# One wait for the four tensors of a turn, one for each half of attention's transposes, in TensorE's queue

## The chip, the cores and the metric

The program runs on one core of a Trainium2 chip (trn2). The metric is device time in microseconds (us) of one execution, shown as the median of a few. The core has five engines with a queue of instructions each: TensorE (PE; its weight loads are shown as PEld), VectorE (DVE), ScalarE (ACT), GpSimd (POOL) and SyncE (SP), which only issues transfers. They meet through semaphores: an instruction that is done adds one to a counter, and a queue that waits for a value stands still until the counter has it, with all that is behind it.

## What is computed

The reference runs two transformer blocks over one sequence of 1024 tokens with 1024 features, all in float32. What matters here is the first block's mixer, which has two branches from the same input:

```python
def one_block(args):                       # latent attention, 8 heads, 96 features per head
    s = (jnp.einsum('bqhd,bkhd->bhqk', qn_b, k_nope)
         + jnp.einsum('bqhd,bkd->bhqk', qr_b, k_rope))
    p = jax.nn.softmax(s.astype(jnp.float32) * scale, axis=-1)
    return jnp.einsum('bhqk,bkhd->bqhd', p.astype(v.dtype), v)
...
def step(state, inp):                      # wkv7 recurrence, 8 heads of 64, run forward and backward
    sa = jnp.einsum('bhvk,bhk->bhv', state, a_t)
    state = (state * w_t[:, :, None, :] + sa[..., None] * b_t[:, :, None, :]
             + v_t[..., None] * k_t[:, :, None, :])
    return state, jnp.einsum('bhvk,bhk->bhv', state, r_t)
```

The rest (input projections, output projections, gated feed-forward, a second block with a 31-tap convolution and a squared-relu MLP) is dense matrix work that the change does not touch.

## The kernel before

The kernel is one program, written engine by engine: every function ends in the engine that it writes for (`_pe`, `_dve`, `_act`, `_pool`, `_sp`), and each engine's queue is filled in the order of the calls. Nothing is reordered by a tool. `X.up(...)` names the increment that an instruction makes when done, and `e.wait_ge(*X.by(...))` waits for it. There is one counter for each engine and part (`v` is VectorE's and `a` ScalarE's of one direction of the recurrence, `t_at`, `v_at`, `a_at` are attention's), so waiting for a later increment of an engine covers all its earlier ones.

The stage in question, `scan_pe` and its fellows, runs from about 525 to 1195 us. It interleaves three programs by a fixed table of slots (`slots`, with the orders written out in `STEADY`, `HEAD`, `ENDING`):

- direction 0 and direction 1 of the recurrence (`w_pe`, `w_dve`, ...), each in 8 steps of 128 tokens, so 16 half steps. A half step is a chain of calls: `split`, `cum`, `mul`, `turn`, `scores`, `PV`, `Nc`, the `row`s, `spread`, `X`, `Y3` to `X5`, `WU`, `RG`, `OH`, `S0`, `S1`, `post1` to `post3`. Direction 1 is 13 slots behind direction 0.
- attention (`att_pe`, ...), 64 units of one head and 128 queries: `S` (scores, line 1784), `M` and `R` on VectorE (maximum, reciprocal), `E` and `P` on ScalarE (exponential, scaling, into `Pb`), `T0` and `T1` on TensorE (four transposes of `Pb` each, line 1807, into `bank[6]`), `C0` and `C1` on ScalarE (copies into `PT`, lines 1824 and 1839), `V` (line 1795).

In `cum`, TensorE makes the running sums of the decays (lines 1367 to 1370) and ScalarE their exponentials (lines 1518 to 1527). In `mul`, VectorE makes four 128x512 tensors one after the other: At (line 1589), Rt (1594), Bt (1596) and Kt (1597). In `turn`, TensorE transposes each by four 128x128 transposes (line 1379), 16 in all, and in ScalarE's `turn` the results are copied to SBUF (lines 1536 and 1541). `scores` (line 1392) needs those copies.

The recurrence's results go through `wring`, a ring of four PSUM banks that both directions share. `wtake` takes the next bank, and waits until whoever read that bank's last content is done (line 1342). A turn takes all four banks. For direction 1 those four are left by `OH` and `cum` of its own step; for direction 0 they are left by its `cum` (three) and by direction 1's `X`, whose four copies ScalarE makes (line 1352), and that one is the bank of Kt. In direction 1's first step the fourth bank is left by direction 0's matmuls of line 1433, which VectorE adds up (line 1654).

In front of a matmul one wait can sit on the weight load itself; every further one becomes an instruction of its own in TensorE's queue, EVENT_SEMAPHORE, which holds up to two waits. By the profile's operands the wait written first is the one on the weight load, and the later ones become EVENT_SEMAPHOREs in front of it.

Of the kernel before, what the change touches and what calls it, by code (L numbers as in the profile page):

```python
# [213 lines left out]
def build(nc, A, out):  # L214
# [3 lines left out]
    def sb(name, kb, shape, dt=F32):  # L218
        return nc.alloc_sbuf_tensor_at(name, shape, dt, offset=base + int(kb * 1024))
# [6 lines left out]
    def signals(name):  # L226
        everything.append(Signals(nc, name))
        return everything[-1]
# [9 lines left out]
    def hs(h):  # L238
        return slice(512 * h, 512 * (h + 1))
# [1099 lines left out]
    def wtake(e, d, s, name, *empties):  # L1339
        ap, waits = wring.take((d, s, name), *empties)  # L1340
        for w in waits:
            e.wait_ge(*w)
        return ap
# [11 lines left out]
    def w_pe(e, d, s, c):  # L1355
        x, t, v, a, g = D[d], t_w[d], v_w[d], a_w[d], g_w[d]
# [13 lines left out]
                m = e.matmul(b2[:, 2 * p:2 * p + 2], sg[:, 128 * p:128 * (p + 1)], K("ones2", 2), start=True, stop=True)  # L1370
            m.then_inc(*t.up(s, "D"))
        if c == "turn":
            for name, sig, empty in (("At", v, a), ("Rt", v, a), ("Bt", v, a), ("Kt", v, a)):
                ap = wtake(e, d, s, name, (empty, s, name + "T"))
                e.wait_ge(*sig.by(s, name))
                for p in range(4):
                    src = {"At": x.AP[:, p, 0, :], "Bt": x.SC[:, p, 4, :, :].rearrange("t h c -> t (h c)"), "Rt": x.Rt[:, 128 * p:128 * (p + 1)],
                           "Kt": x.Kt[:, 128 * p:128 * (p + 1)]}[name]
                    m = e.transpose(ap[:, 128 * p:128 * (p + 1)], src, ident)  # L1379
                m.then_inc(*t.up(s, name))  # L1380
# [14 lines left out]
        if c == "PV":  # L1395
            e.wait_ge(*v.by(s, "SC", 1, 1))
            ap = wtake(e, d, s, "PV", (a, s, "PV"))
# [6 lines left out]
        if c == "X":  # L1404
            ap = wtake(e, d, s, "X", (a, s, "X", 3))
            e.wait_ge(*v.by(s, "XT0"))
            across_pe(e, ap, x.XT).then_inc(*t.up(s, "X"))
        if c in ("Y3", "Y4", "Y5"):
# [5 lines left out]
            ap = wtake(e, d, s, ("Y", lev), (v, s, "Y", lev))  # L1414
# [5 lines left out]
            if lev > 3:  # L1420
                ap = wtake(e, d, s, ("XT", lev - 1), (a, s, "XT", lev - 1, 3))
                across_pe(e, ap, x.X).then_inc(*t.up(s, "XT", lev - 1))
        if c in ("X3", "X4", "X5"):
# [5 lines left out]
            if lev < 5:  # L1429
                ap = wtake(e, d, s, ("X", lev), (v, s, "X", lev))  # L1430
# [5 lines left out]
            else:  # L1436
                ap = wtake(e, d, s, ("XT", lev), (v, s, "XT", lev))
# [47 lines left out]
        if c in ("S0", "S1"):  # L1485
# [8 lines left out]
            ap = wtake(e, d, s, ("S", n), (v, s, "S+", n))  # L1494
# [255 lines left out]
    PT = sb("PT", 24, [128, 8, 2, 128])  # L1750
# [7 lines left out]
    t_at, v_at, a_at = signals("t_at"), signals("v_at"), signals("a_at")  # L1758
# [15 lines left out]
    def att_pe(e, u, c):  # L1774
        g, k, j, h = u // 2, u // 16, (u // 2) % 8, u % 2
        if c == "S":
            if u % 16 == 0:
                e.wait_ge(*d_kp.by(k))
            if h == 0:
                e.wait_ge(*d_qb.by(g))  # L1780
            if u:
                e.wait_ge(*a_at.by("E", u - 1))
            for half in range(2):
                m = e.matmul(bank[4 + half], Qb[g % 3][:, h, :], Kp[k % 2][:, h, hs(half)], start=True, stop=True)  # L1784
            m.then_inc(*t_at.up("S", u))
        if c == "V":
            w = g - 1
            e.wait_ge(*a_at.by("PT", 2 * w + 1))
            if w % 8 == 0:
                e.wait_ge(*d_vp.by(w // 8))  # L1790
            if w % 4 == 0 and w:
                e.wait_ge(*a_at.by("O", w - 1))
            for i in range(8):
                for n in range(2):
                    m = e.matmul(bank[7][64 * n:64 * n + 64, 128 * (w % 4):128 * (w % 4) + 128],  # L1795
                                 Vp[(w // 8) % 2][:, i, 64 * n:64 * n + 64], PT[:, i, n, :], start=i == 0, stop=i == 7)
            m.then_inc(*t_at.up("O", w))
        if c in ("T0", "T1"):
            w, n = u - 1, int(c[1])
            e.wait_ge(*a_at.by("P", w))  # L1800
            if n:
                e.wait_ge(*a_at.by("PT0", w))
            elif w:
                e.wait_ge(*a_at.by("PT", w - 1))
            for q in range(4):
                i = 4 * n + q
                m = e.transpose(bank[6][:, 128 * q:128 * (q + 1)], Pb[w % 2][:, 128 * i:128 * (i + 1)], ident)
            m.then_inc(*t_at.up("PT", w, n))
# [166 lines left out]
    def scan_pe(e):  # L1975
        e.wait_ge(*v_pre.all())
        e.wait_ge(*a_pre.all())
        e.wait_ge(*v_gt.all())
        scan(e, "pe", w_pe, att_pe, tail_pe)
# [1500 lines left out]
```

## Time and profile before

| | us |
|---|---|
| median of the runs shown (3155.31 to 3159.33) | 3156.21 |
| the profiled execution | 3153.93 |
| its span, first to last instruction | 3152.1 |
| TensorE busy | 3069.7 (97%) |
| VectorE busy | 2026.5 (64%) |
| ScalarE busy | 1136.5 (36%) |
| mean granted TensorE clock | 0.992 of full |

Times in the rows are in us from the span's start unless marked ns. A busy TensorE is not one at its peak: matmuls overlap, so a row's length is longer than its share of the queue. What a group costs is the distance from its start to the next group's start.

### The profile page before, as it was taken

How to read it: one execution, taken by the hardware profiler on the slowest of the kernel's cores; microseconds unless marked ns; L12 is line 12 of the kernel's file. 1: busy time of each engine (PE TensorE's matmuls, PEld its weight loads, DVE VectorE, ACT ScalarE, POOL GpSimd, SP SyncE). 2: the span in 40 equal slices, each digit the busy share in tenths (PEclk: the TensorE clock that was granted, in tenths of full speed). 3: DMA queues.
4: the chain of work that ended last, by engine and by line, in shares of the span. 5: the costliest groups of instructions: out<-in, count | busy, mean ns of one | idle time of the engine just before them, and what ended most of it. 6: DMA issues, size and time to landing. Idle time of an engine off the chain costs nothing.

```text
span 3152.1 us, 52318 instructions
## 1 busy us (share of the span) xinstructions
PE 3069.7 (97%) x22008; PEld 2495.9 (79%) x22008; DVE 2026.5 (64%) x3073; ACT 1136.5 (36%) x1691; POOL 448.5 (14%) x488
## 2 busy tenths in 40 slices
PE   8999999899999999999999999999999999999999
PEld 7887887677777777888888888888766887788887
DVE  6665554477777765546555565788887888664454
ACT  5222334566666653223222222201154233433232
POOL 0232442011111100402222212101000000200000
PEclk9999999999999999999999999999999999999999
DMA  4332766223232222425455553666411222223322
GB/s 151 127 133 84 229 224 205 67 78 95 78 93 73 81 99 92 154 86 220 175 197 196 195 200 134 253 240 264 176 67 54 94 97 90 94 94 121 107 94 80
DMA packets 121754, 424.98 MB, mean 135 GB/s; under 512 B 15536, under 2 KB 41776, under 8 KB 94128
## 3 DMA queue, kind: packets, MB, share of 16 engines
q1 hardware_dynamic: 86880, 295.26, 26.6%
q0 software_dynamic: 34640, 126.37, 10.9%
q8 instruction: 175, 2.87, 0.4%
q14 instruction: 59, 0.48, 0.0%
HBM read 311.48 MB, written 110.10 MB: 134 GB/s over the span
## 4 chain that ended last, share of the span: by engine, by line
PE 81%; DVE 11%; issue 2%; ACT 2%; POOL 2%; DMA 1%; SPq 0%; DVEq 0%; ACTq 0%; POOLq 0%
PE ps L2634 30%; PE ps L321 14%; PE ps L505 7%; PE ps L2442 4%; PE ps L1784 3%; PE ps L2344 3%; PE ps L1417 2%; PE ps L2158 2%; PE ps L1379 1%; DVE st_m L1813 1%; PE ps L1433 1%; PE ps L1795 1%; PE ps L2801 1%; PE ps L1026 1%; DVE Yh L2823 1%
## 5 line engine op out<-in xcount | busy, mean ns | idle before, releaser
L293 ACT ACTIVATE whi<-raw 128x2048 fp32r<-128x2048 f32 x131 | 250.5, 1912 | 389.0 <-PE ps L2634 195.3
L297 DVE TENSOR_TENSOR wlo<-raw,whi 128x2048 fp32r<-128x2048 f32 x131 | 301.7, 2303 | 86.0 <-ACT whi L293 85.7
L2823 DVE SCALAR_TENSOR_TENSOR Yh<-uT,vc,Yh 128x512 f32<-128x512 f32 x448 | 326.2, 765 | 3.2
L2634 PE MATMUL ps<-Hh,whi 128*128 128x512 f32 x1024 | 316.9, 391 | 0.6 <-DVE wlo L297 0.6
L2634 PEld LDWEIGHTS ps<-Hh,whi 128*128 128x128 f32 x1024 | 192.2, 188 | 42.5 <-issue 1.9
L321 PE MATMUL ps<-Hlo,whi 128*128 128x512 f32 x672 | 206.9, 389 | 0.0
L321 PE MATMUL ps<-Hhi,wlo 128*128 128x512 f32 x672 | 206.9, 389 | 0.0
L321 PE MATMUL ps<-Hhi,whi 128*128 128x512 f32 x672 | 206.8, 389 | 0.0
L2634 PE MATMUL ps<-aHh,whi 128*128 128x512 f32 x512 | 199.5, 390 | 2.3 <-DVE wlo L297 2.2
L2634 PE MATMUL ps<-Hh,wlo 128*128 128x512 f32 x512 | 199.2, 389 | 0.0
L2634 PE MATMUL ps<-aHh,wlo 128*128 128x512 f32 x512 | 199.2, 389 | 0.0
L2634 PE MATMUL ps<-aLh,whi 128*128 128x512 f32 x512 | 199.2, 389 | 0.0
L3001 DVE TENSOR_TENSOR xT<-ps,xT 128x512 f32<-128x512 f32 x256 | 168.8, 682 | 20.4 <-PE ps L2634 20.4
L2634 PE MATMUL ps<-Gh,whi 128*128 128x512 f32 x576 | 180.8, 395 | 0.0
L505 PE MATMUL ps<-Hhi,whi 128*128 128x512 f32 (+1 forms) x512 | 163.5, 401 | 0.0
L505 PE MATMUL ps<-Hlo,whi 128*128 128x512 f32 (+1 forms) x512 | 158.7, 391 | 0.0
L505 PE MATMUL ps<-Hhi,wlo 128*128 128x512 f32 (+1 forms) x512 | 158.3, 390 | 0.0
L2987 DVE TENSOR_TENSOR aLh<-rth,aHh 128x512 fp32r<-128x512 f32 x64 | 43.0, 713 | 164.1 <-ACT aHh L2981 164.1
L321 PEld LDWEIGHTS ps<-Hhi,wlo 128*128 128x128 f32 x672 | 126.2, 188 | 26.2
L321 PEld LDWEIGHTS ps<-Hlo,whi 128*128 128x128 f32 x672 | 126.2, 188 | 26.1
L321 PEld LDWEIGHTS ps<-Hhi,whi 128*128 128x128 f32 x672 | 126.2, 188 | 26.1
L1784 PE MATMUL ps<-Kp,Qb 96*128 96x512 f32 x256 | 125.9, 614 | 5.9 <-ACT Pb L1829 4.5
(415 smaller groups left out, 6470.0 us busy)
## 6 DMA issues: line engine op xcount, KB each, us to landing
raw<-in_panels SPq DMA_DIRECT2D x131, 1024.0 KB, 4.8
whi<-sph SPq DMA_DIRECT2D x28, 1024.0 KB, 4.8
wlo<-spl SPq DMA_DIRECT2D x28, 1024.0 KB, 6.9
rwf<-F POOLq DMA_DIRECT2D x16, 1280.0 KB, 6.7
sraw<-in_panels POOLq DMA_DIRECT2D x40, 512.0 KB, 4.5
sph<-shi POOLq DMA_DIRECT2D x40, 512.0 KB, 4.5
spl<-slo POOLq DMA_DIRECT2D x40, 512.0 KB, 5.2
L<-rwf SPq DMA_DIRECT2D x16, 1024.0 KB, 5.0
```

What stands on the lines that cost most here:

```text
L293: e.activation(whi[i % 2][:, :], raw_of(i)[:, :], AF.Copy).then_inc(*a_hi.up(i))
L297: e.tensor_tensor(wlo[i % 2][:, :], raw_of(i)[:, :], whi[i % 2][:, :].bitcast(F32), OP.subtract).then_inc(*v_lo.up(i))
L321: m = e.matmul(aps[h][0:n1 - n0, :], w[wi][:, kc, n0:n1], mov[mi][:, kc, hs(h)], start=x == 0 and q == 0, stop=x == len(kcs) - 1 and q == 2)
L505: m = e.matmul(aps[h][0:n1 - n0, :], W[wi][:, kc, n0:n1], H2[mi][:, kc, hs(h)], start=kc == 0 and q == 0, stop=kc == 7 and q == 2)
L1417: m = e.matmul(ap[cols(cc_), 32 * i:32 * (i + 1)], x.SC[cols(cc_), p, BA, h, :], part(x.X[cols(cc_), i, :], lev, d), start=True, stop=True)
L1784: m = e.matmul(bank[4 + half], Qb[g % 3][:, h, :], Kp[k % 2][:, h, hs(half)], start=True, stop=True)
L2158: m = e.matmul(aring.bank("ya", n, h), W[wi][:, k, n0:n0 + 128], (oahi, oalo)[mi][:, k, hs(h)], start=k == 0 and q == 0, stop=k == 3 and q ...
L2344: m = e.matmul(aps[h], W[wi][:, kc, n0:n0 + 128], H2[mi][:, kc, hs(h)], start=kc == 0 and q == 0, stop=kc == 7 and q == 2)
L2442: m = e.matmul(ap, W[wi][:, kc, 128 * n:128 * n + 128], (aH, aL)[mi][b % 2][:, kc, :], start=kc == 0 and q == 0, stop=kc == 1 and q == 2)
L2634: m = e.matmul(ap, W[wi][:, kc, n0:n0 + 128], mov[mi][:, kc, :], start=x == 0 and q == 0, stop=x == len(kcs) - 1 and q == 2)
L2823: e.scalar_tensor_tensor(out=to, in0=x, scalar=w, in1=to, op0=OP.mult, op1=OP.add).then_inc(*v_e.up(*key))
L3001: e.tensor_tensor(xT[:, n, hs(h)], ring.bank("x", h, b, n), xT[:, n, hs(h)], OP.add).then_inc(*v_e.up("x", h, b, n))
```

## The change

Two places in TensorE's queue. In `turn`, the four waits for At, Rt, Bt and Kt, one in front of each tensor's transposes, become one wait for Kt, the last that VectorE makes, in front of all; and all four banks are taken ahead of the first transpose instead of one by one. In `T0` and `T1`, the wait for `P` goes where a later increment of the same counter is waited for anyway. The instructions that compute, their order and the data are the same.

```diff
         if c == "turn":
-            for name, sig, empty in (("At", v, a), ("Rt", v, a), ("Bt", v, a), ("Kt", v, a)):
-                ap = wtake(e, d, s, name, (empty, s, name + "T"))
-                e.wait_ge(*sig.by(s, name))
+            e.wait_ge(*v.by(s, "Kt"))
+            aps = {name: wtake(e, d, s, name, (a, s, name + "T")) for name in ("At", "Rt", "Bt", "Kt")}
+            for name, ap in aps.items():
                 for p in range(4):
...
         if c in ("T0", "T1"):
             w, n = u - 1, int(c[1])
-            e.wait_ge(*a_at.by("P", w))
             if n:
                 e.wait_ge(*a_at.by("PT0", w))
-            elif w:
-                e.wait_ge(*a_at.by("PT", w - 1))
+            else:
+                e.wait_ge(*(a_at.by("PT", w - 1) if w else a_at.by("P", w)))
```

## Rows read from the trace of the kernel before

**Rows 1.** The page, part 1: busy time of each engine.

```profile
PE 3069.7 (97%) x22008; PEld 2495.9 (79%) x22008; DVE 2026.5 (64%) x3073; ACT 1136.5 (36%) x1691; POOL 448.5 (14%) x488
```

**Rows 2.** Busy time by stretch: length, each engine busy (instructions), granted clock, DMA share, GB/s.

```profile
591.00:1158.00 567.00, 545.98 (x9840) 434.20 (x9839) 395.52 (x866) 348.12 (x663) 53.42 (x75) 1.00 0.26 78
```

**Rows 3.** Waits of TensorE, 525 to 1155 us: in total, times, longest.

```profile
PE ps L1807 <- ACT PT L1839: 4.0, 8, 0.5
PE ps L1807 <- ACT PT L1824: 3.9, 5, 0.8
PE ps L1379 <- DVE AP L1589: 3.9, 7, 1.0
```

**Rows 4.** Timeline of a turn of direction 1: start, length, instructions.

```profile
737.67 0.68 DVE L1589 SCALAR_TENSOR_TENSOR AP<-L,E 128x512 f32<-128x512 f32 x1
738.50 0.63 PE L1379 MATMUL ps<-cc,AP 128*128 128x128 f32 x4 [0.22 <-DVE AP L1589]
739.47 0.68 DVE L1597 TENSOR_TENSOR Kt<-L,E 128x512 f32<-128x512 f32 x1
740.30 0.63 PE L1379 MATMUL ps<-cc,Kt 128*128 128x128 f32 x4
740.76 0.60 PE L1807 MATMUL ps<-cc,Pb 128*128 128x128 f32 x4
741.20 1.02 PE L1784 MATMUL ps<-Kp,Qb 96*128 96x512 f32 x2
```

**Rows 5.** Timeline of the stage's first turn, direction 0.

```profile
534.95 0.60 PE L1379 MATMUL ps<-cc,AP 128*128 128x128 f32 x4
...
536.70 0.60 PE L1807 MATMUL ps<-cc,Pb 128*128 128x128 f32 x4
```

**Rows 6.** Timeline of a later turn of direction 0.

```profile
699.36 1.59 ACT L1352 ACTIVATE X<-ps 64x256 f32<-64x256 f32 x4
699.48 0.66 PE L1379 MATMUL ps<-cc,AP 128*128 128x128 f32 x4 [0.22 <-ACT E L1523]
...
700.30 0.68 DVE L1597 TENSOR_TENSOR Kt<-L,E 128x512 f32<-128x512 f32 x1
701.13 0.63 PE L1379 MATMUL ps<-cc,Kt 128*128 128x128 f32 x4
...
701.72 0.48 PE L1417 MATMUL ps<-X,SC 64*64 64x32 f32 x10
```

**Rows 7.** The stage's second turn, direction 1, in the timeline.

```profile
588.86 1.11 PE L1379 MATMUL ps<-cc,AP 128*128 128x128 f32 x4
```

**Rows 8.** Wait instructions of lines 1375 and 1802: ns min/median/max, first and last.

```profile
L1375 PEldq EVENT_SEMAPHORE  x63: 51/51/51, 534.5 to 1143.5; - x63
L1802 PEldq EVENT_SEMAPHORE  x64: 51/51/51, 530.8 to 1149.6; - x64
```

**Rows 9.** Timeline: VectorE and TensorE waiting for each other, and a starved group of transposes.

```profile
744.18 2.48 DVE L1602 TENSOR_TENSOR SC<-ps,cc 128x512 f32<-128x512 f32 x4 [2.19 <-PE ps L1392]
...
746.72 1.15 PE L1401 MATMUL ps<-L,SC 64*64 64x64 f32 x32 [0.70 <-DVE SC L1602]
...
725.70 0.69 DVE L1662 COPY WU<-ps 128x512 f32<-128x512 f32 x1 [1.80 <-PE ps L1450]
...
726.16 0.63 PE L1807 MATMUL ps<-cc,Pb 128*128 128x128 f32 x4 [0.51 <-ACT PT L1839]
```

**Rows 10.** The chain that ended last, in order of time: start, length, what.

```profile
738.50 2.43 PE ps L1379 x16
```

**Rows 11.** Two long gaps of TensorE, in the timeline.

```profile
562.52 2.29 PE L1784 MATMUL ps<-Kp,Qb 96*128 96x512 f32 x4 [2.49 <-ACT Pb L1829]
...
2685.61 0.50 PE L2634 MATMUL ps<-aHh,whi 128*128 128x512 f32 x1 [1.84 <-DVE wlo L297]
```

**Rows 12.** Busy time by stretch behind those gaps; the clock is the third number from the end.

```profile
564.00:567.40 3.40, 3.40 (x28) 2.66 (x28) 2.04 (x3) 0.40 (x1) 1.46 (x3) 0.51 0.10 29
2685.50:2689.00 3.50, 3.39 (x15) 2.81 (x16) 3.06 (x4) 2.79 (x3) 2.84 (x2) 1.00 0.71 225
```

## The prediction

> **What bounds the kernel now.** I read the page's busy times first. TensorE is busy 97% of the span [rows 1], so whatever keeps its queue standing is paid in full unless a later wait shrinks by as much. Then the stretches: in the 567 us from 591 to 1158 us, where 14 of the 16 turns and nearly all of attention lie, TensorE is busy 546 us at full granted clock, VectorE 396 and ScalarE 348 [rows 2]. Only 21 us are idle there, and the list of waits names a few places; two of them are the places of this change: the transposes of At wait for VectorE's first multiplication, and attention's transposes wait for ScalarE's copies [rows 3].
>
> Then the timeline around a turn. The reader is to compare the times at which VectorE's multiplications start with the times at which TensorE's groups of four transposes start. In a turn of direction 1, At's multiplication starts at 737.67 and ends at 738.35, and the transposes start at 738.50; Kt's starts at 739.47 and ends at 740.15, and its transposes start at 740.30 [rows 4]. TensorE follows VectorE 0.15 us behind, tensor by tensor: three groups from 738.50 to 740.30 are 0.60 us apart, VectorE's pace. The first turn shows TensorE's own pace, since the multiplications were long done: four groups take 536.70 - 534.95 = 1.75 us, 0.44 each [rows 5]. Seven turns look like rows 4, seven like those of direction 0 [rows 6], and two, the first of each direction, find all four tensors ready [rows 5, 7].
>
> Last, the chain that ended last. It runs through the turn, 16 transposes in a row [rows 10], with VectorE's multiplication of At ahead of it and attention's and the scores' matmuls behind it.
>
> **The change part by part: the turn.** The new wait sits in front of At and ends when Kt is ready. So the 12 transposes of At, Rt and Bt, which TensorE now makes while VectorE works on the next tensor, all come behind Kt's multiplication.
>
> Direction 1: Kt is ready at 740.15 [rows 4]. How soon the first transpose follows: 0.15 us where the wait is an instruction of its own, as now; 0.06 where a single wait sits on the weight load (VectorE's fourth result ends at 744.18 + 2.48 = 746.66, the matmul starts at 746.72 [rows 9]). By the rule of the program's operands the wait for Kt, written first, now sits on the load, so I take 0.09, and 0.06 to 0.15 as bounds. First transpose at 740.24, 1.75 us for 16, next group at 741.99. Before, it started at 740.76. The loss is 1.23 us (1.20 to 1.29).
>
> Direction 0: Kt is ready at 700.98 [rows 6]. The bank for Kt is held by direction 1's X, whose copies end at 699.36 + 1.59 = 700.95, which before held back only Kt's group and now holds back all; it ends just before Kt does, so it adds nothing here, but the two are in a dead heat. Start 0.12 us behind, 701.10, then 1.75 us, and 0.09 for the change of shape in front of the 64x64 group (701.72 - 701.13 = 0.59 against 0.44 plus waiting): 702.94 against 701.72. The loss is 1.22.
>
> Fourteen turns at 1.23 us are 17.2 us. The stage's first turn loses nothing. In the second, the bank that Kt takes is left by matmuls right in front of it, so the transposes, which started at 588.86 [rows 7], now wait for a VectorE addition: 0.4 to 0.8 us, I take 0.6.
>
> What hides it: nothing that I can find. Behind the turn stand attention's T1 and S, then the scores, and those are followed by a VectorE wait of 2.19 us and by TensorE's next wait of 0.70 us for VectorE's products [rows 9]. Both hang on TensorE's own scores and move with them. ScalarE's copies of a turn now start about 1 us later, still in front of the scores that read them, because the four 512-column matmuls of S stand between [rows 4], or the small matmuls of line 1417 in direction 0 [rows 6]. VectorE's next multiplications are no fixed point either: 12 us ahead of them, at 725.70, VectorE stood 1.80 us waiting for TensorE's matmuls of line 1450 [rows 9] and worked on from there almost without a gap, so it moves with TensorE and at the next turn the same wait is met again. The transfer that reloads the inputs waits for Bt and Kt, which don't move. The bounds are full price, and half of it if some later wait gives way.
>
> **The waits themselves.** Dropped from the turn: three waits on VectorE. Four banks are waited for by two instructions ahead. That is 63 instructions less and about 32 more. Dropped in attention: 64 + 63 = 127. Each instruction lasts 51 ns [rows 8]. Are they paid? In rows 4 the group at 740.76 has two waits in front, and it starts 0.46 us behind the last; a group with nothing late takes 0.44 [rows 5]. TensorE's queue reads the waits while earlier matmuls still run, so a wait that is over costs 0 to 0.02 us: I take nothing. Where the wait is late, it stands in the way: removal moves the release from a separate instruction onto the load, 0.05 us (one instruction) to 0.09 us (0.15 less 0.06). That applies to the starved groups, 8 + 5 in the list of waits [rows 3] (one of them is the group at 726.16 [rows 9]) and, as an estimate, one more that waits for P. 14 x 0.07 = 1.0 us gained. Upper bound of this part: all of 158 - 32 less at 51 ns, taken under the last rival.
>
> Beside this, the Trainium skill ("Advanced Engine Details and Errata", Network/Comms) gives 50 to 100 ns for a sequencer to read a semaphore. By it, if nothing overlapped, 127 reads would be an estimated 6 to 13 us; the 0.46 against 0.44 us above speaks against that here.
>
> **TensorE's clock.** A turn's gap grows: in direction 1 from 0.22 or 0.96 to some 2.0 or 2.7 us, in direction 0 to 1.8 us behind one group of four transposes. Gaps of that size are on either side of trouble: behind the one of 2.49 us that ended at 562.52 the granted clock was half (1.2 instead of 2.4 GHz) for some 3.4 us, behind the one of 1.84 us that ended at 2685.61 it stayed full [rows 11, 12]. Between the two lie all of the new gaps, with thin work around those of direction 0. A stretch of 3.4 us at half clock costs at most 1.7 us; the row of four transposes at 588.86, in another such stretch, is 1.11 us long against 0.60 at full clock [rows 5, 7]; not all of 3.4 us is such work, so I take 1.5 us. I expect 5 of the 14 turns to be hit: 7.5 us; bounds 0 and 14 x 1.7 = 24 us.
>
> The Trainium skill ("Perfetto Trace Analysis", Matmul Optimizations) says that the engine "dynamically scales power based on utilization", so that matmuls should run back to back in batches. A batch of 16 in place of four of four looks like that advice, but the gap in front is longer than all it closes; the rows above carry the price.
>
> **Sum.** 17.2 + 0.6 - 1.0 + 7.5 = 24.3 us. On the profiled execution's own 3153.93 that is 3178.2. The median of the runs is 2.28 us above it, so 3180.5.
>
> **Rivals.**
> - *The delay alone.* The new gaps leave the clock at full: 3156.2 + 16.8 = 3173.0. For it: the clock is 1.00 over 567 us although gaps up to 1.0 us are in it. Against: the row of 2.49 us.
> - *Nearly every turn loses the clock.* 16.8 + 22 = 3195.
> - *The delay is absorbed.* Later waits of TensorE give way by half: 3156 + 8 = 3164, fully: 3156. For it: 0.70 and 0.51 us waits exist. Against: they hang on TensorE's own work, and the chain goes through the turn.
> - *Other side: the waits cost their 51 ns, and turns lose nothing.* Then 127 + 31 = 158 instructions at 0.051 us are 8.1 us, 3148. It decides only if VectorE had Kt ready when TensorE comes to the turn, as in rows 5; in 14 turns of 16 Kt is 1.6 us or more late. A mechanism that is there only in the two first turns.
>
> **How the numbers follow.** Delay with some clock loss 55%, delay alone 25%, nearly every turn at half clock 7%, absorbed 8%, waits dear and turns free 5%. The range leaves out the last and the deep end of absorption: 3168 (delay alone with a quarter absorbed) to 3196. Slower by over 0.2% is all but the last two, and a part of absorption: 92%; within 0.2% (6.3 us, about what a measurement can tell from no change) 4%; faster 4%.
>
> **What would show it.** In every turn of rows 4 and 6 the first transpose starts just behind the end of Kt's multiplication and the 16 run 0.44 us a group; the wait of TensorE at line 1379 grows from about 5 us in total to 25 to 30, by VectorE's Kt (line 1597). The next groups are 1.2 us later against VectorE's At than before. Starved groups of line 1807 start 0.05 to 0.09 us sooner after ScalarE. The page's clock line and the stretch from 591 to 1158 us show the half clock as a mean below 1.00: five stretches are 0.985. The rest of the program, from 1196 us on, takes as long as before. I am wrong if the stage does not lengthen (some wait gives way that I took to hang on TensorE), if the transposes start before Kt is ready, or if X's copies in direction 0 end later than Kt and hold all 16 back still more.

## The result and the profile after

The changed kernel is slower: 3176.10 us, median of 4 runs (3170.79 to 3184.63), against 3155.76 for the kernel before (4 runs, 3150.22 to 3159.33). The ratio is 1.0062, 95% interval 1.0044 to 1.0081. Five more runs later, beside the last experiment, gave 3174.83 against 3153.92, ratio 1.0068 [1.005, 1.0085]. The forecast was 3180.5, range 3168 to 3196. The profiled execution took 3170.79, its span is 3169.0.

The page, part 1, of the kernel after. TensorE is busy 3.5 us less than in [rows 1], in a span 16.9 us longer, so it stands idle 20.4 us more:

```profile
PE 3066.2 (97%) x22008; PEld 2498.1 (79%) x22008; DVE 2026.0 (64%) x3073; ACT 1137.1 (36%) x1691; POOL 447.9 (14%) x488
```

Waits of TensorE in the kernel after, 525 to 1175 us (total, times, longest). The diff makes all later lines of TensorE one smaller, so line 1806 is line 1807 of before, and so on:

```profile
PE ps L1379 <- DVE Kt L1597: 29.0, 14, 2.7
...
PE ps L1806 <- ACT PT L1823: 3.4, 5, 0.7
PE ps L1806 <- ACT PT L1838: 2.9, 7, 0.4
...
PE ps L1379 <- DVE X L1654: 0.6, 1, 0.6
```

Where [rows 3] had 3.9 us for At in 7 turns, there are now 29.0 us for Kt in 14. The two waits for ScalarE's copies went down from 4.0 and 3.9 us to 2.9 and 3.4. The second turn waits 0.6 us for an addition of VectorE.

A turn of direction 1 in the kernel after, timeline, to be laid beside [rows 4]:

```profile
829.54 0.68 DVE L1597 TENSOR_TENSOR Kt<-L,E 128x512 f32<-128x512 f32 x1
...
830.28 0.66 PE L1379 MATMUL ps<-cc,AP 128*128 128x128 f32 x4 [2.02 <-DVE Kt L1597]
...
830.77 0.60 PE L1379 MATMUL ps<-cc,Rt 128*128 128x128 f32 x4
...
831.21 0.60 PE L1379 MATMUL ps<-cc,SC 128*128 128x128 f32 x4
...
831.64 0.60 PE L1379 MATMUL ps<-cc,Kt 128*128 128x128 f32 x4
...
832.08 0.60 PE L1806 MATMUL ps<-cc,Pb 128*128 128x128 f32 x4
```

Kt's multiplication ends at 830.22. The first transpose starts 0.06 us behind it, the next group 1.86 us behind it. In [rows 4] that group started 0.61 us behind Kt's end (740.76 - 740.15), so the turn loses 1.25 us. A turn of direction 0, as the chain of the work that ended last passes through it (start, length, what):

```profile
786.58 0.51 DVE AP L1589
...
787.18 0.40 DVE Rt L1594
...
787.78 0.69 DVE SC L1596
788.47 0.61 DVE Kt L1597
789.08 0.08 issue
789.16 1.94 PE ps L1379 x16
791.10 0.99 PE ps L1417 x30
```

In [rows 10] VectorE's part of the chain ended with At; now it runs through all four multiplications and only then come the sixteen transposes. TensorE and VectorE, which worked side by side, work one behind the other.

The same instruction of VectorE can be found in both traces by its number in the queue. The distance between the two, from one instruction to the next, shows where time is lost. Worked out from the two traces, 620 to 1150 us of before:

```
start before  start after  step us  turn of direction
   622.86        624.27     +2.90     0   (and +1.51 more up to 627)
   664.25        668.43     +1.25     1
   702.88        709.90     +2.84     0
   744.18        752.40     +1.25     1
   782.74        792.20     +1.25     0
   824.07        835.50     +1.26     1
   862.62        876.89     +2.83     0
   903.94        920.99     +2.85     1
   942.49        962.38     +2.84     0
   984.53       1005.62     +1.25     1
  1023.81       1047.73     +2.84     0
  1066.07       1090.97     +1.24     1
  1105.43       1133.09     +2.83     0
  1145.76       1174.64     +1.29     1
```

Fourteen steps, each at a turn. Seven are the delay alone, 1.25 us. In the other seven half clock stands behind it and costs some 1.6 us more (2.84 - 1.25), at the first of them 3.2. Apart from one of 0.75 us (a gap of TensorE at 797.20 for which the trace names no wait) nothing else in this stretch stays that is larger than about 0.3 us. The sum is 14 x 1.25 = 17.5 for the delay, 6 x 1.59 + 3.2 = 12.7 for the clock, and 0.75: 31 us (the distance itself goes from -1.5 at 620 us to +28.9, so small steps give back 0.6). Of the 28.9, 16.9 are left at the end. By TensorE's own instructions the distance falls to 19.4 at 1196 us: the kernel before had its own stretches of half clock from 1158 us on, 27 us long in all, the kernel after only 6.8 there, and 20.5 us less of half clock can be worth up to 10.2. The other 2.5 go at about 1313 us, where TensorE stands 2.2 us waiting for VectorE (line 2344) in the kernel before and not at all in this execution. The second trace of the changed kernel has a wait of 2.3 us there again, so the change doesn't bring that gain.

Timeline of one of the seven turns with half clock, and busy time by stretch of two of them and of the turn shown above (length, each engine busy, granted clock third from the end):

```profile
914.17 1.12 PE L1379 MATMUL ps<-cc,AP 128*128 128x128 f32 x4 [2.02 <-DVE Kt L1597]
...
915.07 1.06 PE L1379 MATMUL ps<-cc,Rt 128*128 128x128 f32 x4
```

```profile
914.00:917.40 3.40, 3.23 (x15) 3.24 (x16) 1.75 (x7) 1.57 (x3) 1.45 (x3) 0.51 0.71 216
1043.80:1047.20 3.40, 3.40 (x34) 3.07 (x32) 0.00 (x0) 2.78 (x5) 0.00 (x0) 0.50 0.91 296
830.00:833.40 3.40, 3.12 (x23) 2.64 (x24) 1.87 (x7) 2.43 (x5) 1.45 (x3) 1.00 0.73 243
```

The two turns at 914 and at 830 have the same gap of 2.02 us in front. The reader is to see that one of them is followed by half clock (0.51 of full, 1.2 GHz) and the other by full clock: the length of the gap alone does not decide it. At half clock the groups of a turn stand 0.85 to 0.90 us apart instead of 0.44.

### The profile page after: what moved, and what is told of

Same layout as the page of the kernel before. It is cut to its first block, busy times and chain, and to the rows that moved or that the text cites. A ratio compares the mean times of both kernels' runs of the same rounds, so it can differ in the third digit from the quotient of the medians.

```text
span 3169.0 us, 52160 instructions
## 1 busy us (share of the span) xinstructions
PE 3066.2 (97%) x22008; PEld 2498.1 (79%) x22008; DVE 2026.0 (64%) x3073; ACT 1137.1 (36%) x1691; POOL 447.9 (14%) x488
## 4 chain that ended last, share of the span: by engine, by line
PE 81%; DVE 12%; issue 2%; ACT 2%; POOL 1%; DMA 1%; SPq 0%; DVEq 0%; ACTq 0%; POOLq 0%
PE ps L2633 30%; PE ps L321 14%; PE ps L505 7%; PE ps L2441 4%; PE ps L2343 3%; PE ps L1784 3%; PE ps L1417 2%; PE ps L2157 1%; PE ps L2280 1%; PE ps L1379 1%; DVE st_m L1812 1%; PE ps L2800 1%; PE ps L1026 1%; DVE Yh L2822 1%; PE ps L1795 1%
```

## The experiments

Each kernel was timed in turns with the kernel before on the same chip; the medians of the latter stand beside each.

**Attention's waits alone.** The turn is as before; only the edit in `T0` and `T1` is made.

```diff
-            e.wait_ge(*a_at.by("P", w))
             if n:
                 e.wait_ge(*a_at.by("PT0", w))
-            elif w:
-                e.wait_ge(*a_at.by("PT", w - 1))
+            else:
+                e.wait_ge(*(a_at.by("PT", w - 1) if w else a_at.by("P", w)))
```

> Only the waits of T0 and T1 are changed; the turn is that of the kernel before. Late-Kt theory (the turn's twelve transposes behind Kt cost the time): this part is worth 0.05 to 0.09 us for each of some 14 starved groups, so 1 us less than before, within what can be told from no change; the 943 ns gaps of attention's second group in the first steps shrink by 0.09 us. Rival (each wait instruction costs its 51 ns): 127 instructions, 6.5 us faster. Rival (something in attention's waits made the changed kernel slow): 10 us or more slower.

3155.18 us (12 runs, 3144.73 to 3159.89) against 3158.16; ratio 0.9995 [0.9977, 1.0012]. Its waits, 525 to 1175 us:

```profile
PE ps L1379 <- DVE AP L1589: 4.3, 7, 1.0
...
PE ps L1806 <- ACT PT L1823: 3.4, 5, 0.7
PE ps L1806 <- ACT PT L1838: 2.9, 7, 0.4
```

127 wait instructions of 51 ns [rows 8] are gone, 6.5 us if they were paid one by one, and by the ratio the time went down by 1.6 us (0.05%), inside an interval that reaches to 7.3 us gained; the fit below narrows it to 0.8 +- 1.5. What is gained is seen at the starved groups: those that wait for the second copy stood 4.0 us in 8 places [rows 3], now 2.9 in 7; one by one, seven of them wait 0.42 instead of 0.51 us and five of those for the first copy 0.69 instead of 0.78, in sum 12 x 0.09 = 1.1 us. The turn waits for At as before. This half of the change is free of harm and nearly of use.

**The turn alone.** Attention's waits are as before, the turn as after.

> Only the turn is changed; attention's waits are those of before. Late-Kt theory: as the changed kernel plus 1 us, so some 20 us slower than before, 1.25 us at each of 14 turns and the rest from stretches at half clock. Rival (attention's waits made the difference): within 6 us of before.

3185.60 us (6 runs, 3169.55 to 3187.72) against 3158.16; ratio 1.0091 [1.0059, 1.0123]. The turn alone has the whole loss. That it comes out 9 us above the whole change goes with the mean granted clock of its runs, 0.9877 against 0.9898; at equal clock the two are 16.2 +- 2.2 and 14.9 +- 1.8 us above the kernel before (table below).

**All four banks first, each tensor with its own wait.**

```diff
-            for name, sig, empty in (("At", v, a), ("Rt", v, a), ("Bt", v, a), ("Kt", v, a)):
-                ap = wtake(e, d, s, name, (empty, s, name + "T"))
-                e.wait_ge(*sig.by(s, name))
+            aps = {name: wtake(e, d, s, name, (a, s, name + "T")) for name in ("At", "Rt", "Bt", "Kt")}
+            for name, ap in aps.items():
+                e.wait_ge(*v.by(s, name))
```

> All four banks are taken ahead of the first transpose, but each tensor keeps its own wait on VectorE. Late-Kt theory: nothing lost in direction 1 (its banks are free long before), and in direction 0 everything waits for ScalarE's copies of X, which end with Kt, so 7 turns x 1.25 = 8.8 us and part of the half-clock stretches, since six of the seven stretches behind turns came in direction 0: 9 to 18 us slower. Rival (taking banks early costs nothing, only the wait for Kt does): within 3 us of before. Rival (the banks are the whole cost): as the changed kernel, +20 us.

3179.59 us (6 runs, 3168.51 to 3193.92) against 3158.16; ratio 1.0082 [1.005, 1.0113]. First its waits, then a turn of direction 0 in its timeline:

```profile
PE ps L1379 <- DVE Kt L1597: 13.5, 7, 1.9
...
PE ps L1379 <- DVE AP L1589: 3.9, 7, 1.0
```

```profile
699.36 0.63 PE L1379 MATMUL ps<-cc,AP 128*128 128x128 f32 x4 [1.94 <-DVE Kt L1597]
...
699.82 0.60 PE L1379 MATMUL ps<-cc,Rt 128*128 128x128 f32 x4
```

The profile names VectorE's Kt in front of At's transposes, though nothing in this kernel waits for Kt there. What holds the queue is Kt's bank, which is left by ScalarE's copies of direction 1's X 0.01 to 0.04 us before Kt's multiplication ends, the dead heat of the prediction; the list of waits names the one that came last. Direction 0 loses 1.37 us in each of seven turns, 0.12 more than with the wait for Kt, since the first transpose starts 0.21 us behind Kt's end and not 0.10. Direction 1 has the same instructions with banks that are long free, follows VectorE as before and loses nothing, which leaves the bank as the cause. So taking the banks ahead is a fault of its own: in direction 0 it delays as much as the wait for Kt does, and the two together cost no more than one. The clock fell behind four of the seven, three times for 10.2 us at a stretch, as behind one turn of one other kernel; the traces give no reason for it.

**One wait for Kt, the banks one by one.**

```diff
-            e.wait_ge(*v.by(s, "Kt"))
-            aps = {name: wtake(e, d, s, name, (a, s, name + "T")) for name in ("At", "Rt", "Bt", "Kt")}
-            for name, ap in aps.items():
+            for name in ("At", "Rt", "Bt", "Kt"):
+                if name == "At":
+                    e.wait_ge(*v.by(s, "Kt"))
+                ap = wtake(e, d, s, name, (a, s, name + "T"))
```

(The minus lines are the kernel after; attention is as before.)

> One wait for Kt ahead of the turn, but the banks are taken one by one as before. Late-Kt theory: as the turn of the changed kernel within 2 us, since Kt is later than every bank: some 20 us slower than before. Rival (the banks taken ahead cost): clearly faster than the changed kernel.

3173.85 us (6 runs, 3171.78 to 3183.91) against 3155.12; ratio 1.0064 [1.0043, 1.0085]. All fourteen turns have the step of 1.25 us, four of them with half clock behind (+2.8). Its wait for Kt, to be laid beside the 29.0 us of the changed kernel:

```profile
PE ps L1380 <- DVE Kt L1598: 28.1, 14, 2.7
```

The wait for Kt alone gives the whole delay.

**Two waits, for pairs.** As the last, but waiting for Rt ahead of At and Rt, and for Kt ahead of Bt and Kt.

```diff
-                if name == "At":
-                    e.wait_ge(*v.by(s, "Kt"))
+                if name in ("At", "Bt"):
+                    e.wait_ge(*v.by(s, "Rt" if name == "At" else "Kt"))
```

> Two waits in the turn: one for Rt ahead of At and Rt, one for Kt ahead of Bt and Kt; banks one by one. Late-Kt theory: eight transposes instead of four lie behind Kt, 0.44 us less 0.06 to 0.09, so 0.36 us a turn, 14 x 0.36 = 5 us, and gaps are too short for the clock to fall: 5 us slower than before. Rival (any merged wait costs the clock and the same 1.25 us): 15 to 20 us slower. Rival (fewer wait instructions pay): not slower.

3158.62 us (12 runs, 3153.92 to 3165.24) against 3158.16; ratio 1.0007 [0.999, 1.0024]. A turn of direction 1 in its timeline (lines one larger than before):

```profile
739.15 0.66 PE L1380 MATMUL ps<-cc,AP 128*128 128x128 f32 x4 [0.74 <-DVE Rt L1595]
...
739.64 0.60 PE L1380 MATMUL ps<-cc,Rt 128*128 128x128 f32 x4
...
740.35 0.42 PEld L1380 LDWEIGHTS ps<-cc,SC 128*128 128x128 f32 x4 [0.35 <-DVE Kt L1598]
740.35 0.66 PE L1380 MATMUL ps<-cc,SC 128*128 128x128 f32 x4
...
740.85 0.60 PE L1380 MATMUL ps<-cc,Kt 128*128 128x128 f32 x4
...
741.29 0.60 PE L1808 MATMUL ps<-cc,Pb 128*128 128x128 f32 x4
```

Kt's multiplication ends at 740.30; behind it come two groups instead of one, and the step is 0.33 to 0.38 us at thirteen turns, and 1.64 at the one behind which the clock fell. Before, one group comes behind the last tensor; with two the turn loses 0.37 us, with four 1.25, so the two further groups cost (1.25 - 0.37) / 2 = 0.44 us each, their own time.

**Kt earlier on VectorE.** The kernel after, with attention's maximum `M` moved one slot later in VectorE's order.

```diff
-        "dve": {... 12: "1 0 R", 13: "1 0 M", 15: "1 0 R",
+        "dve": {... 12: "1 0 R", 13: "1 0", 14: "1 0 M", 15: "1 0 R",
```

> The changed kernel with VectorE's maximum for attention placed behind the four multiplications of direction 1 instead of ahead of them, so that Kt is ready 1.14 us sooner there. Late-Kt theory: the wait at direction 1's turns shrinks from 2.0 to 0.9 us, and its price with it, 7 turns x about 1 us, 5 to 8 us faster than the changed kernel, unless the later maximum delays attention's exponential and with it the next scores by as much. Rival (the price does not hang on how late Kt is): as the changed kernel or slower.

3180.33 us (6 runs, 3172.71 to 3185.42) against 3155.12; ratio 1.0077 [1.0055, 1.0099]. Its waits, and the timeline behind a turn:

```profile
PE ps L1379 <- DVE Kt L1597: 20.8, 14, 1.8
PE ps L1784 <- ACT Pb L1828: 11.5, 12, 2.3
```

```profile
741.07 0.66 PE L1379 MATMUL ps<-cc,AP 128*128 128x128 f32 x4 [0.89 <-DVE Kt L1597]
...
742.87 0.60 PE L1806 MATMUL ps<-cc,Pb 128*128 128x128 f32 x4
...
744.63 1.95 PE L1784 MATMUL ps<-Kp,Qb 96*128 96x512 f32 x4 [1.16 <-ACT Pb L1828]
```

The wait for Kt fell by 8.2 us, and the wait of the scores `S` for the exponential, which hangs on that maximum, grew by 6.9 (4.6 to 11.5). At equal clock (below) the kernel is 17.8 +- 2.1 us above the kernel before, not less than the changed kernel's 14.9 +- 1.8. The delay can be moved to another wait by this reordering of VectorE, but it isn't paid back.

**The gap filled.** The kernel after, with three (direction 0) or four (direction 1) matmuls of 256 columns of a constant written into At's bank in front of the wait for Kt. Nobody reads their result; it only keeps TensorE at work.

```diff
         if c == "turn":
+            aps = {"At": wtake(e, d, s, "At", (a, s, "AtT"))}
+            if s:
+                idle_pe(e, aps["At"][:, 0:256], 4 if d else 3)
             e.wait_ge(*v.by(s, "Kt"))
-            aps = {name: wtake(e, d, s, name, (a, s, name + "T")) for name in ("At", "Rt", "Bt", "Kt")}
+            aps.update({name: wtake(e, d, s, name, (a, s, name + "T")) for name in ("Rt", "Bt", "Kt")})
```

> The changed kernel with matmuls of no use (three in direction 0, four in direction 1, into the bank that At's transposes then overwrite) in the gap ahead of the turn's wait, from the second step on. They are new work, but it lies in time in which TensorE stood still. Theory (each turn costs 1.25 us by itself, and about 1.6 us more where the granted clock falls to half behind the gap): the clock stays at full through the turns, so some 8 to 12 us faster than the changed kernel and 17 us slower than before. Rival (the clock falls for another reason, or the fall costs nothing because work is waiting anyway): as the changed kernel. Rival (the filling delays the transposes): slower than the changed kernel.

3174.89 us (6 runs, 3170.11 to 3179.78) against 3155.12; ratio 1.0058 [1.0039, 1.0077]. Thirteen turns had a step of 1.25 to 1.29 us. At one the clock fell at 1120.5 us, and there the useless matmuls, at half clock, held the transposes back until 1.22 us behind Kt (step 2.65); the stage otherwise behaved as expected of the clock theory, the whole program did not get 8 us faster, and in this trace 41 us of half clock stood near the stage's ends. So it was run once more, beside the changed kernel as it is, to see what the clock costs end to end:

> The changed kernel as it is, timed more often and beside its variant with the gap filled, on one chip. It asks how much of the end-to-end difference is granted clock. If the clock lost behind seven turns is a net cost (12.7 us in the profiled stage), the changed kernel is some 17 + 8 to 13 us, 25 to 30, above the kernel before, and its variant with filled gaps 8 to 12 us below it. If the stretches at half clock are about as many in sum whatever the turns do (others take their place or fall away elsewhere), both are 17 to 20 us above the kernel before and within 3 us of each other.

> The variant with the gap filled (three or four 256-column matmuls whose result nobody reads, in front of the wait for Kt), timed more often beside the changed kernel. Net clock theory: 8 to 12 us below the changed kernel, ratio to the kernel before 1.0053 to 1.0058 with the changed kernel's at 1.008 or more. Theory that the sum of half-clock stretches hardly depends on the turns: both ratios at 1.0055 to 1.0065.

The changed kernel took 3174.83 us (5 runs, 3172.75 to 3178.96), the variant 3170.87 (6 runs, 3165.07 to 3181.74), the kernel before 3153.92; ratios 1.0068 [1.005, 1.0085] and 1.0059 [1.0037, 1.0081]. Busy time and clock from 620 to 1163 us, first of the changed kernel's profile shown above, then of the variant:

```profile
620.00:1163.00 543.00, 506.58 (x8991) 408.06 (x8989) 362.66 (x795) 319.45 (x605) 48.51 (x67) 0.97 0.25 76
```

```profile
620.00:1163.00 543.00, 524.79 (x9204) 419.89 (x9206) 371.39 (x812) 325.40 (x619) 51.49 (x71) 1.00 0.26 78
```

In the variant's trace all fourteen turns have the step of 1.25 us (1.25 to 1.29) and none has half clock behind it; in the second trace of the changed kernel six have (five of direction 0, one of direction 1), each +2.8. So the two are separate: the delay stays when the clock is kept. End to end the difference of the medians is 4 us, between the 8 to 12 of one theory and the under 3 of the other, and with ranges this wide neither is excluded by these two alone.

What the traces of all kernels say together on the clock behind a turn, with the granted clock of each turn read from its trace (two traces of the changed kernel and of the filled one, one of each other):

```
turns                                                  number   half clock behind
wait for Kt ahead, direction 0, gaps of 1.7 to 1.8 us    35        24
wait for Kt ahead, direction 1, gaps of 0.9 to 2.8 us    35         2
   of these, gaps of 2.5 to 2.8 us                       12         0
gaps short or filled, both directions                    70         3
```

The first three rows are the changed kernel, the turn alone, the banks one by one and Kt earlier; the last is the kernel before, attention's waits alone, the two waits and the filled gap. So the merged wait does bring the half clock, but the length of its gap doesn't say where: the longest gaps, in direction 1, never did. The three in the last row are all in direction 0.

**All runs together.** Every run lists its mean granted clock, so time can be split into what goes with the clock and what doesn't. A least squares fit over 114 runs (the first four of the changed kernel and all of the experiments and of the kernel before beside them), with one slope for the clock and one offset for each kernel (+- is twice the standard error):

```
kernel                    runs  mean clock  offset at equal clock, us   by the clock, us
before                     45     0.9917        0                         0
after                       9     0.9898      +14.9 +- 1.8              +5.2
gap filled                 12     0.9913      +16.2 +- 1.5              +1.1
banks one by one            6     0.9903      +16.9 +- 2.1              +3.8
turn alone                  6     0.9877      +16.2 +- 2.2             +10.9
banks first                 6     0.9852       +5.9 +- 2.5             +17.8
Kt earlier                  6     0.9897      +17.8 +- 2.1              +5.5
two waits                  12     0.9918       +2.9 +- 1.5              -0.3
attention's waits alone    12     0.9920       -0.8 +- 1.5              -0.8
slope: 2.74 us for 0.001 of mean clock; what is left over: 2.4 us (standard deviation)
```

The last column is the difference of mean clocks times 2736 us. The clock is rounded to 0.001 in each run, so a single one is worth little and only the means count; for nine runs the last column is known to about +- 3.4 us. The four kernels with the merged wait and an unfilled gap have a mean clock of 0.9894 over 27 runs, the four with short or filled gaps 0.9917 over 81: a difference of 0.0023 +- 0.0009, or 6.3 +- 2.4 us. That settles what the pair of kernels alone left open: half clock behind the turns is a net cost, some 6 us where 8 to 12 were expected. The offsets have a weakness: the one for the banks first, whose clock lies farthest out, is 5.9, while its trace has 7 x 1.37 = 9.6 us of steps. With an offset more for each round of runs, the changed kernel's own becomes 16.7 +- 2.5.

## Why the prediction was right, and where it was off

- **The delay of a turn.** Predicted 1.23 us, measured 1.25 in turn after turn. TensorE starts 0.06 us behind Kt in direction 1 and 0.10 in direction 0 (0.09 and 0.12 assumed), and in direction 1 the sixteen transposes take 1.80 instead of 1.75 us, since the first group behind a wait is 0.49 long, not 0.44.
- **What hides it: nothing.** Right. Fourteen steps, none given back by a later wait in the stage; each goes on to VectorE's multiplications of the next turn. At equal clock the changed kernel is 14.9 +- 1.8 us slower and its variant 16.2 +- 1.5, against 17.2 + 0.6 - 1.0 = 16.8 predicted. The absorbed rival (8 or 0 us) is out.
- **The dead heat of X's copies and Kt.** Right, and shown by the kernel with the banks first, where X's copies alone hold all sixteen back in direction 0 for 1.37 us.
- **The second turn.** It waits 0.6 us for VectorE's addition, as predicted. It starts at 588.33 against 588.86 in [rows 7], but that one stood in a stretch of half clock, so the two can't be compared for what it costs. The kernel with two waits takes its banks one by one and has full clock there: over the same instructions around that turn it needs 0.5 us less than both traces of the changed kernel.
- **The waits themselves.** A wait that is over costs next to nothing: right. The count of 158 instructions less (127 + 31) holds, so the upper bound's "158 - 32" takes the 32 new ones off twice; the rival uses 158. Paid at 51 ns the 127 of attention would have been 6.5 us; at equal clock 0.8 +- 1.5 were gained. The rival on the other side is out twice, as all fourteen turns lost their 1.25 us. The Trainium skill ("Advanced Engine Details and Errata", Network/Comms) with its 50 to 100 ns for reading a semaphore would give an estimated 6 to 13 us for those 127, if nothing overlapped; the runs, at 0.8 +- 1.5 us, don't show that. The starved groups: 14 at 0.07 us predicted, 12 at 0.09 measured; the group of [rows 9] waits 0.42 instead of 0.51.
- **TensorE's clock.** The term that was mis-sized, in ways that partly cancel. Predicted: 5 of 14 turns at 1.5 us, 7.5 us. In the traces 7 and 6 turns were hit, at 1.6 us, once 3.2: 12.7 us in the first. What was missing in the prediction is that stretches of half clock at the stage's ends are different in every execution, and that the kernel before has its share of them, 10 us at 581 and 27 us from 1158 on in its profiled run. Over all runs of the changed kernel the net is +5.2 us, +- 3.4. The forecast's 3180.5 is 4.4 us above the median of the first runs; by these figures 2.3 of it are the clock (7.5 - 5.2) and 1.9 the delay (16.8 - 14.9), the first within its uncertainty, the second at the edge of it. The measure that the prediction went by, the length of the gap, failed. It had all new gaps between 1.84 us (full clock) and 2.49 us (half), but its own 2.7 us of direction 1 lie above both, and the three of 2.74 to 2.75 us in this trace kept the clock, while six of the seven of 1.8 us in direction 0 lost it. That the count of 5 came near 7 and 6 is in part luck. Direction 0 is hit far more often than direction 1 (11 of 14 turns in the two traces against 2 of 14), where the prediction named thin 64x64 work; no run tested that by itself.
- **The rivals' order.** Delay alone (3173.0) is 3.1 us from the first median and 1.8 from the second, closer than the forecast (4.4 and 5.7). The traces show that it isn't the mechanism as such, since the clock fell behind six and seven turns, but as a number it was the better one. Nearly every turn (3195) is out.
- **Signs named ahead.** The wait at line 1379 of 25 to 30 us: 29.0. The stage's mean clock: 0.97 from 620 to 1163, below the 0.985 named. From 1196 us on unchanged: nearly. TensorE is 19.4 us behind at 1196 and 16.9 at the end, and the difference is the wait at 1313 us that this execution lacks and the second one has.

The Trainium skill's advice ("Perfetto Trace Analysis", Matmul Optimizations) to run matmuls back to back in batches would have spoken for this change: sixteen transposes are one batch now. Here the batch had to be paid with a gap of some 2 us in front, and behind 7 and 6 of the fourteen turns of the two traces the granted clock fell to half.

Open: why the clock falls behind one gap of 2.02 us and not behind another, and behind most gaps of direction 0 and hardly any of direction 1; why the kernels with the turn alone and with the banks first lose more clock than the others (0.9877 and 0.9852), with six runs each; and the gap of 0.57 us at 797.20 without a wait.

## What to carry to other kernels

A wait that is over when the queue reaches it is free, so taking it out earns nothing; merging waits into the last one is free only where all producers have long finished. Where consumer and producer go tensor by tensor at the same pace, one wait for the last puts all but one of the consumer's groups behind it, and the price is the consumer's own time for those groups, here 3 x 0.44 us a turn. The same holds for a resource that is taken ahead of its use: a ring's bank taken three tensors early holds back the three that had theirs. Before an edit of this kind, compare when each of the merged conditions is met, not how many waits there are.

## What had not been expected of the hardware

- The granted clock fell behind 24 of 35 gaps of 1.7 to 1.8 us in direction 0, behind 2 of 35 in direction 1 and behind none of the twelve longest of those (2.5 to 2.8 us). It fell behind one gap of 2.02 us (914.17) and stayed full behind another (830.28), in the same kernel with the same instructions around them.
- A few matmuls nobody needs, put into the gap, kept the clock at 1.00 over 543 us in one trace and at thirteen turns of fourteen in the other. End to end the mean clock of the runs is 0.0015 higher, some 4 us and by itself not clear of noise, since the program's other stretches of half clock came and went.
- Single runs of one kernel lie up to 24 us apart (3144 to 3168 for the kernel before), and 2.7 us of it go with each 0.001 of mean clock; at equal clock 2.4 us are left as spread.
